# Three more projection chunks and one low-rank chunk split in two fp32r parts, with the low part made by an adding DMA; four output-weight loads start later

## The reference

```python
h = rmsnorm(x, mix_norm[l])
p = h @ w_in[l]                      # first mixer: 1024 -> 3080 columns
...
q, k, v = ...                        # conv + silu of p's columns, then the chunked delta rule
x = x + jnp.concatenate([y_a, y_b], axis=-1) @ w_out[l]

xx = _token_shift(h) - h             # rwkv
xr, xw, xk, xv, xa, xg = [h + xx * mu[i] for i in range(6)]
r = (xr @ w_r).astype(f32)
k = (xk @ w_k).astype(f32)
v = (xv @ w_v).astype(f32)
g = jax.nn.sigmoid(xg @ g1) @ g2     # the last low-rank matrix is g2
...                                  # state recurrence over 256 tokens, 16 heads of 64
return (y * g) @ w_o, v_first
```

## Time and profile before

| | us |
|---|---|
| median of 3 runs | 1241.04 |
| lowest, highest | 1239.42, 1241.42 |
| the profiled execution | 1240.83 |
| its span | 1239.0 |

### The profile page before, as it was taken

The page is one execution under the profiler, slowest core; times in us unless marked ns, Lnnn a source line. Parts: engine busy times, 40 slices in busy tenths (PEclk is TensorE's granted clock), DMA queues, the critical chain, the costliest instruction groups (busy, mean ns, idle before and its releaser), DMA issues.

```text
span 1239.0 us, 23375 instructions
## 1 busy us (share of the span) xinstructions
PE 1221.4 (99%) x9764; PEld 1068.0 (86%) x9764; DVE 538.5 (43%) x821; ACT 618.2 (50%) x812; POOL 777.3 (63%) x195
## 2 busy tenths in 40 slices
PE   8999999999999999999999999999999999999998
PEld 7888887888988888899898888888888998888887
DVE  4232234655333233343523332358968645422233
ACT  6554443445554444585555444464422455644442
POOL 3988880253388888766379888833034425788884
PEclk9999999999999999999999999999999999999999
DMA  7555554243255555553245555532442013555551
GB/s 294 214 189 203 176 197 147 103 172 138 101 188 199 191 200 177 202 193 140 99 139 206 200 187 186 203 136 106 165 167 76 4 37 129 178 204 183 190 201 70
DMA packets 30588, 200.97 MB, mean 162 GB/s; under 512 B 3376, under 2 KB 5296, under 8 KB 6832
## 3 DMA queue, kind: packets, MB, share of 16 engines
q1 hardware_dynamic: 27776, 195.59, 44.1%
q10 hardware_dynamic: 2736, 4.26, 1.0%
HBM read 197.75 MB, written 2.10 MB: 161 GB/s over the span
## 4 chain that ended last, share of the span: by engine, by line
PE 92%; DVE 3%; ACT 1%; issue 1%; POOL 1%; DMA 1%; SPq 0%; POOLq 0%; DVEq 0%
PE psum L351 25%; PE psum L353 13%; PE psum L342 10%; PE psum L344 10%; PE psum L343 10%; PE psum L984 6%; PE psum L997 3%; PE psum L2955 1%; POOL wlo L3303 1%; PE psum L2822 1%; PE psum L339 1%; PE psum L341 1%; PE psum L340 1%; PE psum L2971 1%; PE psum L2841 1%
## 5 line engine op out<-in xcount | busy, mean ns | idle before, releaser
L3303 POOL TENSOR_TENSOR wlo<-raw,whi 128x2048 fp32r<-128x2048 f32 x161 | 741.2, 4609 | 356.9 <-ACT whi L312 308.6
L351 PE MATMUL psum<-f_both,whi 128*128 128x512 f32 x1408 | 492.2, 393 | 1.9 <-DVE wlo L697 1.9
L312 ACT ACTIVATE whi<-raw 128x2048 fp32r<-128x2048 f32 x160 | 306.3, 1915 | 220.5 <-PE psum L353 169.4
L353 PE MATMUL psum<-f_both,wlo 128*128 128x256 f32 x1408 | 393.7, 280 | 0.0
L351 PEld LDWEIGHTS psum<-f_both,whi 128*128 128x128 f32 x1408 | 264.3, 188 | 60.6 <-DVE wlo L697 2.5
L353 PEld LDWEIGHTS psum<-f_both,wlo 128*128 128x128 f32 x1408 | 264.5, 188 | 1.5
L342 PE MATMUL psum<-whi,ahi 128*128 128x512 f32 x352 | 137.4, 390 | 0.3 <-POOL wlo L3303 0.3
L344 PE MATMUL psum<-whi,alo 128*128 128x512 f32 x352 | 137.0, 389 | 0.0
L343 PE MATMUL psum<-wlo,ahi 128*128 128x512 f32 x352 | 136.9, 389 | 0.0
L907 DVE TENSOR_TENSOR psum<-psum,arena 128x512 f32<-128x512 f32 x43 | 30.1, 700 | 241.8 <-ACT arena L623 241.7
L923 DVE TENSOR_TENSOR alo<-arena,ahi 128x512 fp32r<-128x512 f32 x44 | 95.1, 2162 | 31.7 <-ACT ahi L856 31.7
(11 more groups left out here) (416 smaller groups left out, 1534.6 us busy)
## 6 DMA issues: line engine op xcount, KB each, us to landing
raw<-stream SPq DMA_DIRECT2D x182, 1024.0 KB, 4.8
con<-consts SPq DMA_DIRECT2D x1, 1376.0 KB, 14.7
x<-x_in SPq DMA_DIRECT2D x1, 1024.0 KB, 5.1
raw<-stream SPq DMA_DIRECT2D x2, 512.0 KB, 7.5
kept_x<-x ACTq DMA_DIRECT2D x1, 1024.0 KB, 3.9
x<-kept_x ACTq DMA_DIRECT2D x1, 1024.0 KB, 4.7
out<-x SPq DMA_DIRECT2D x4, 256.0 KB, 2.0
arena<-gm_w_s ACTq DMA_DIRECT2D x1, 512.0 KB
```

The costliest lines, as they stand in the source:

```text
L312: nc.scalar.activation(whi[:, slot, :], raw[:, c % RAW, :], ACT.Copy).then_inc(high_made, 1)
L351: nc.tensor.matmul(psum[:, bank, :].rearrange("p (a n) -> p a n", a=2), whi[w], f_both[:, :, k, :], start=k == 0, stop=False, skip_group_c ...
L353: return nc.tensor.matmul(psum[:, bank, 0:TOK], wlo[w], f_hi[:, k, :], start=False, stop=k == KT - 1, skip_group_check=True)
L3303: nc.gpsimd.tensor_tensor(part(wlo[:, slot, :]), part(raw[:, c % RAW, :]), part(whi[:, slot, :]).bitcast(F32), ALU.subtract)\
```

## The change

Four chunks, `w_in` 8, `rw` 1, `rw` 2 and `lora` 2, form the list `SUMMED`. The first three were plain and are now in three passes; `lora` 2 was in three passes already. Their low part is no longer made by POOL's subtraction: ACT writes the rounded chunk to `whi` and the rounded chunk times -1 to `wlo`, and POOL issues one DMA that reads the chunk again from HBM and adds it to `wlo`. The place in `raw` is free after ACT's second write. Order and places change with it: r goes 1, 2, 0, 3, and the chunk of r 1 is loaded before the low-rank ones; the halves of r's input (`r_hi` by ACT, `r_lo` by DVE) are new; in the first mixer `hhi` and `hlo` come earlier; DVE does two of four `unit_kk` later and `mix_variant(5)` earlier. The load of `rw_o` 2 now waits for `y_late(2)` of the recurrence, and with it all loads behind it. Semaphores `idle_filled`, `x_kept` and `x_back` are merged into others.

```diff
-RWKV_ORDER = [("rw", 0, j) for j in (5, 6, 4, 7)] + [("lora", 0, 0), ("lora", 0, 1)] + \
-    [("rw", 0, j) for j in (0, 1, 2, 3, 8)] + [("lora", 0, 2)] + [("rw", 0, j) for j in (9, 10, 11)] + [("rw_o", 0, j) for j in range(4)]
+RWKV_ORDER = [("rw", 0, j) for j in (5, 6, 4, 7, 1)] + [("lora", 0, 0), ("lora", 0, 1)] + \
+    [("rw", 0, j) for j in (2, 3, 0, 8)] + [("lora", 0, 2)] + [("rw", 0, j) for j in (9, 10, 11)] + [("rw_o", 0, j) for j in range(4)]
+SUMMED = [("w_in", 0, 8), ("rw", 0, 1), ("rw", 0, 2), ("lora", 0, 2)]
+R_ORDER = (1, 2, 0, 3)
...
+        def summed_highs(eng, c):
+            slot = SLOT[c]
+            eng.wait_ge(raw_loaded[c % RAW], 16 * (c // RAW + 1))
+            eng.wait_ge(chunk_used, slot_used(c))
+            nc.scalar.activation(whi[:, slot, :], raw[:, c % RAW, :], ACT.Copy).then_inc(s("sum_highs"), 1)
+            nc.scalar.activation(wlo[:, slot, :], raw[:, c % RAW, :], ACT.Copy, scale=-1.0).then_inc(s("sum_highs"), 1)
...
+            for b in range(4):
+                eng.wait_ge(s("rw_mixed"), mixed(4, 2 * b + 1))
+                nc.scalar.activation(r_hi[:, 2 * b:2 * b + 2, :], variant_x[0][:, 2 * b:2 * b + 2, :], ACT.Copy).then_inc(s("rw_sq"), 1)
...
-            for part in range(2):
-                quarter(eng, RW(0), plain_columns, part, variant_x[0])
+                r_quarter(part)
             second(2)
             second(3).then_inc(chunk_used, 1)
...
-            for j in range(1, 4):
-                project(eng, RW(j), plain_columns, h=variant_x[0])
+            project(eng, RW(2), columns_out, hi=r_hi, lo=r_lo)
+            project(eng, RW(0), plain_columns, h=variant_x[0])
+            project(eng, RW(3), plain_columns, h=variant_x[0])
...
+                elif names[c - RAW] in SUMMED:
+                    sp.wait_ge(s("sum_highs"), 2 * summed(c - RAW))
                 else:
                     sp.wait_ge(low_made, LOWS[c - RAW])
+                if names[c] == ("rw_o", 0, 2):
+                    sp.wait_ge(s("rw_late_sum"), LATE_SUMS[("y", 2)])
...
+            def low_by_sum(c):
+                i = summed(c)
+                pool.wait_ge(s("sum_highs"), 2 * i)
+                if i > 1:
+                    pool.wait_ge(s("low_summed"), 16 * (i - 1))
+                nc.gpsimd.dma_start(wlo[:, SLOT[c], :], stream[c], accum_op=ALU.add).then_inc(s("low_summed"), 16)
```

More of the change, by code:

```diff
@@ L198, in build @@
     PLAIN = {c for name, c in CH.items()
-             if name[0] in ("w_in", "rw") and name not in MIX1_SPLIT + RWKV_SPLIT or name in (("lora", 0, 0), ("lora", 0, 1))}
-    used_after = {("rw", 0, 4): CH[("rw", 0, 5)] - 0.5, ("lora", 0, 2): CH[("rw", 0, 11)] + 0.5, **{("w_out", 0, j): CH[("w_in", 0, 1)] + 0.1 * (j + 1) for j in range(3)}}
+             if name[0] in ("w_in", "rw") and name not in MIX1_SPLIT + RWKV_SPLIT + SUMMED or name in (("lora", 0, 0), ("lora", 0, 1))}
+    used_after = {("rw", 0, 4): CH[("rw", 0, 5)] - 0.5, ("rw", 0, 1): CH[("lora", 0, 1)] + 0.5, ("rw", 0, 3): CH[("rw", 0, 0)] + 0.5, ("lora", 0, 2): CH[("rw", 0, 11)] + 0.5, **{("w_out", 0, j): CH[("w_in", 0, 1)] + 0.1 * (j + 1) for j in range(3)}}
     use_order = sorted(range(NCH), key=lambda c: used_after.get(names[c], c))
@@ L208, in build @@
     SLOT[CH[("rw", 0, 7)]] = SLOT[CH[("rw", 0, 4)]]
-    LOWS = list(itertools.accumulate(int(c not in PLAIN) for c in range(NCH)))
+    SLOT[CH[("rw", 0, 1)]], SLOT[CH[("rw", 0, 2)]] = (SLOT[CH[("rw_o", 0, j)]] for j in (0, 1))
+    SLOT[CH[("lora", 0, 2)]] = SLOT[CH[("rw_o", 0, 2)]]
+    LOWS = list(itertools.accumulate(int(c not in PLAIN and names[c] not in SUMMED) for c in range(NCH)))
     ctx = ExitStack()
@@ L331, in upto @@
                 while self.next <= min(c, NCH - 1):
-                    if self.next not in PLAIN:
+                    if names[self.next] in SUMMED:
+                        summed_highs(self.eng, self.next)
+                    elif self.next not in PLAIN:
                         high(self.eng, self.next)
@@ L1212, in mix1_scalar @@
             nc.scalar.activation(Dm, Dm, ACT.Exp).then_inc(s("m1_dexp"), 1)
+            highs.upto(CH[W_IN(8)])
+            eng.wait_ge(S["h_low"], 8 * n + 8)
+            nc.scalar.activation(hhi[:, :, :], hs, ACT.Copy).then_inc(s("m1_sp_high"), 1)
             copy_x(0)
@@ L1409, in mix1_vector @@
             level(0)
+            eng.wait_ge(s("m1_sp_high"), 3)
+            nc.vector.tensor_tensor(hlo[:, :, :], hs, hhi[:, :, :].bitcast(F32), ALU.subtract).then_inc(s("m1_pads_low"), 1)
             level(1)
@@ L2574, in unit_kk @@
                 steps(nc.vector.tensor_tensor(kk[:, k, :], kk[:, k, :], roots[:, k, :], ALU.mult))
-            mix_variant(1)
-            unit_kk(0)
-            for v in (2, 3, 4):
+            for v in (1, 2):
                 mix_variant(v)
-            for b in range(1, 4):
+            for b in (0, 1):
+                unit_kk(b)
+            for v in (3, 4):
+                mix_variant(v)
+            for b in range(4):
+                eng.wait_ge(s("rw_sq"), 9 + b)
+                k = slice(2 * b, 2 * b + 2)
+                nc.vector.tensor_tensor(r_lo[:, k, :], variant_x[0][:, k, :], r_hi[:, k, :].bitcast(F32), ALU.subtract)\
+                    .then_inc(s("rw_mixed"), 1)
+            for b in (2, 3):
                 unit_kk(b)
@@ L2882, in second, with r_quarter @@
                 return mm
+            def r_quarter(part):
+                c, q = CH[RW(1)], PROJ[RW(1)]
+                if part == 0:
+                    eng.wait_ge(s("low_summed"), 16 * summed(c))
+                    eng.wait_ge(bank_read[6 + q % 2], q // 2)
+                j = part // 2
+                for k in range(4 * (part % 2), 4 * (part % 2) + 4):
+                    if j == 0:
+                        eng.wait_ge(s("rw_mixed"), mixed(4, 7) + k // 2 + 1)
+                    w = (slice(None), SLOT[c], slice(k * 256 + j * P, k * 256 + j * P + P))
+                    mm = three_passes(psum[:, 6 + q % 2, j * 256:(j + 1) * 256], whi[w], wlo[w], r_hi[:, k, :], r_lo[:, k, :], True,
+                                      k == 0, k == KT - 1)
+                if part == 3:
+                    mm.then_inc(chunk_used, 1)
             second(0)
             second(1)
-            eng.wait_ge(s("rw_mixed"), mixed(4, 7))
             for part in range(2):
-                quarter(eng, RW(0), plain_columns, part, variant_x[0])
+                r_quarter(part)
             second(2)
@@ L3325, in _ @@
                         mix1_pool(pool, (3,))
-                    if c not in PLAIN:
+                    if names[c] in SUMMED:
+                        low_by_sum(c)
+                    elif c not in PLAIN:
                         low(c)
```

70 lines of the change are left out of this document (42 added, 28 removed).

## The result

The changed kernel takes 1247.77 us (median of 5 runs, 1246.43 to 1248.97) against 1241.04 for the kernel before (5 runs). The ratio is 1.0058, with a 95% interval of 1.0047 to 1.0068: 0.6% slower. The forecast was 1237.8 and the range ended at 1241.8. The profiled execution took 1246.43.

The account below looks back on a forecast made before the run. PE, busy 99% of the span, was taken as the bound. Terms -2.54 - 1.24 + 0.7 - 0.9 + 0.3 + 0.5 = -3.2 us took the profiled 1240.83 to 1237.6, plus 0.2 for the median: 1237.8, range 1236.0 to 1241.8.

Parts of the forecast that it names:

- PE's own work: Three passes shorten PE's rows: two r chunks save 2.54 us, four quarters of chunk 8 in the first mixer 1.24.
- The adding DMA: Each 1 MB add to wlo takes 8 us, between 4.8 and 10.5, and is hidden at that duration.
- The budgets: Time before PE wants each summed chunk: 14.3 us for w_in 8, 17.7 for r 1; r 2 allows adds of 12.7.
- rival 3: Slower: the add exceeds r 2's budget, the gain gone at 14.3 us; 1246.1 at an add of 16; chance 14%.
- estimate from the Trainium skill: For a 1 MB add: 2.0 + 2 x 2.4 = 6.8 us, hidden too; 4.4 for one plain pass.
- sentence on DVE: In rwkv, DVE's step on r falls from 6.86 to about 3.5 us; DVE is some 2.4 earlier, like PE: 0.
- The first mixer's pauses: PE's 0.63 us pause in the first mixer's levels may grow by 0.5, 0 to 2 (three pauses its size).
- The hold: Holding outputs 2 and 3 gains 0.9 of PE's 1.17 us pause at 946.26 and loses 0.3 near 1008.
- v 9's wait: v 9's load, queued behind lora 2's, makes PE wait 0.7 us after v 8, 0.3 to 1.2.
- the 9.6 of 9.8 us: In rwkv, ACT's new work just fits before its second low-rank activation: 0 lost, up to 0.6 if r 2 lands late.
- the slower case: Add duration beyond r 2's budget, deciding from 14.3 us, where 3.2 us are lost and the gain is gone; chance 14%.

Follow-up runs that it names:

- e4: The changed kernel with its four adding DMAs replaced by plain copies from the same queue, the addition left out: 1243.09 us, ratio 1.0013.
- e5: The kernel of e1 with the adding DMA of lora 2 issued behind POOL's low of output 0: 1238.88 us, ratio 0.9990.
- e1: The changed kernel with the load of w_in 3 held until PE has used w_in 8: 1242.58 us, ratio 1.0012.
- e7: The kernel before with only the load of output 2 held until y_late(2): 1239.12 us, ratio 0.9988.
- e3: The changed kernel without the wait for y_late(2) at the load of output 2: 1252.62 us, ratio 1.0082.
- e2: The changed kernel with an edit to lora 2's add that changed no order, so a second measurement of it: 1248.24 us, ratio 1.0056.
- e12: Adding DMAs for r 1, r 2, late lora 2; output loads and POOL's keys held; v 9 loaded before lora 2: 1238.32 us, ratio 0.9986.
- e8: The kernel of e1 with the four lows made by POOL's subtraction in place of the adding DMAs: 1249.88 us, ratio 1.0067.

## Why the prediction was wrong, point by point

Two steps failed: the price put on the pauses of the first mixer, 0.5 us, and the conclusion that an add for which nobody waits is hidden. The rest of the sum came out nearly as forecast.

- **PE's own work**: right. From the k products at 858.37 to v 8 PE took 44.1 us instead of 46.7, 2.5 less. The quarters of `w_in` 8 became shorter too, but see below.
- **The adding DMA**: 8 us assumed, 10.1 measured in the median, just under the upper bound of 10.5, and 9.2 to 11.7 for the four, so the longest is above the bound. The budgets held: PE waited at no first product of `w_in` 8, r 1 or r 2, and rival 3 did not come about. The prediction's estimate from the Trainium skill (DMA: Bandwidth & Descriptors, section Anatomy of one DMA, and Collectives: The Full Stack, section The bandwidth ceiling) was 6.8; the measured 6.2 for the copy against 4.4 and 10.1 for the add against 6.8 show it low here. Being issued by POOL cost the transfer little: the copies of e4, issued the same way, take 1.4 us more than SP's loads. The step that failed is not the duration but its conclusion, "hidden": I asked only who waits for the add, not which load waits beside it. Output 0's load took 9.1 us instead of 4.8, its `whi` and POOL's low came 6 us late, and that low then stood beside DVE's step. That cost about 3 us: without it PE reached the levels 3.3 us sooner (e5 against e1, from the k products on), and the time fell by 2.7 us by the ratios. The prediction's sentence on DVE, "0", took the gain of POOL's low gone from one step (6.86 to 3.26, right) and missed that the same mechanism had a second place 20 us later.
- **The first mixer's pauses**: the term that failed most. I put 0.5 us (0 to 2) on "chunk 8's place comes free sooner, so that its next load falls there too". The pauses grew by 0.54 at 238.19 (0.38 of it because PE arrived there sooner), by 0.3 at 248.82 and by 2.73 at 253.30, the slow clock behind the last took 1.3, and 0.7 is spread over smaller waits (0.2 of them for POOL's mask, behind a low of chunk 9 that began 1.1 us later): 5.5, less the saving of 1.24, is the 4.3 measured. The direction was named, the size was wrong because the price of a pause was taken from pauses at full clock; what the clock falls to behind a longer pause stood in no row of before. And the three pauses of 0.63 that bounded the term were no bound: PE stands until its instructions are in, and three loads in a row kept them out for about 3 us longer. e1 shows it: 4.6 us in the traces, 5.7 by the medians.
- **The hold**: 0.6 forecast, 1.2 measured on the kernel before (e7), 3.2 in the traces and 4.4 by the medians on the changed one (e3 against e2). Its reading of the gap at 946.26 was right: in the kernel before an instruction transfer moves at 945.26, as the two loads end, and PE resumes 1.2 us after its end. In the changed kernel that gain is inside the 1247.77; without it the loss would be 11 to 12 us.
- **v 9's wait**: 0.7 forecast, 0.6 measured. The sum put the last data of the pair near 908 at 914.95; in finer slices they move by 914.8, which makes the 7.6 us of the pair 7.4. The order that removed it (e12) made another load late and was no faster.
- **ACT**: it waited 0.62 us for its second low-rank activation; the 9.6 of 9.8 us were about right.
- **The rivals**: the slower case was tied to a duration above 14.3 us. That was the wrong mechanism; the case that came true, in which the traffic delays other loads and PE pauses behind them, was folded into the small term of the pauses.

What stays open is the clock. It fell to 0.50 behind pauses of 2.73, 2.46, 1.90 and 1.74 us and stayed at 1.00 behind one of 1.95 (e8); it fell behind PE's wait of 1.7 for DVE (e5) and not behind one of 2.1 (e12). It stayed low for 3.4 us in most places, for 6.8 in one and for 10.2 behind the pauses of e3 and e4. No run says what decides it.

## What to carry to other kernels

When a buffer comes free sooner, follow the load that it releases and look at what PE does behind a burst of loads; here one to three of 1 MB were followed by 1.2 to 3.0 us of standstill, in some places with the lower clock behind it. Where PE stands with no releaser, look at when the transfers of kind "instruction" move in the DMA records. A DMA that nobody waits for still makes its neighbours late: list the loads that it overlaps and who waits for them. Where a step of VectorE with two inputs from SBUF is on the path, look at what GpSimd runs beside it and order that behind.

## What was not expected of the hardware

- An adding DMA of 1 MB takes 10.1 us against 6.2 for a copy from the same queue and 4.8 for a load from SP's.
- A VectorE operation of 0.69 us took 5.02 beside a GpSimd subtraction of 4.52 (e8), and two that take 0.76 together took 5.69.
- All 30 of PE's pauses of 0.25 us or more without a releaser, in 14 traces, end 1.2 to 1.6 us after a 16 KB instruction transfer, and those of 1.7 us or more have that transfer within the last 2.4 us of one to three loads.
- Behind a pause of 2.73 us, and behind PE's wait of 3.3, TensorE ran at a granted clock of 0.50 for 3.4 us; behind a shorter pause, of 1.90 in e4, for 10.2 us; behind the pause of 1.17 in the kernel before it stayed at 1.00.
- The same hold of a load is worth 1.2 us in one kernel and 3.2 to 4.4 in another, since the pause that it removes is followed by the slow clock in the second.
